# Delta rule on unnormalised queries and keys, with decay rows, grams, masks and weight units in another order

## The reference

```python
def l2_normalize(x):
    return x * lax.rsqrt(jnp.sum(x * x, axis=-1, keepdims=True) + EPS)

def gdn_direction(q, k, v, beta, g):
    gc = jnp.cumsum(to_chunks(g), axis=-1)
    decay = jnp.exp(jnp.where(incl, gc[..., :, None] - gc[..., None, :], -jnp.inf))
    kb = kc * bc[..., None]
    lower = jnp.where(strict, einsum("nbhid,nbhjd->nbhij", kb, kc) * decay, 0.0)
    rhs = jnp.concatenate([vc * bc[..., None], kb * jnp.exp(gc)[..., None]], axis=-1)
    sol = lax.linalg.triangular_solve(lower + eye, rhs, left_side=True, lower=True)
    ...
    # step over the chunks, with u, w = the two halves of sol
    v_new = ui - wi @ state
    out = (qi * exp(gi)) @ state + ((qi @ ki.T) * di) @ v_new
    state = state * exp(g_last) + (ki * exp(g_last - gi)).T @ v_new

q = l2_normalize(silu(conv(q))) * 128 ** -0.5;  k = l2_normalize(silu(conv(k)));  v = silu(conv(v))
o = o_f + o_b
o = o * lax.rsqrt(jnp.mean(o * o, axis=-1, keepdims=True) + EPS) * norm_g
```

## Time and profile before

| | |
|---|---|
| median of three runs | 1715.95 us |
| the profiled execution's own time | 1716.34 us |
| its span in the profile | 1714.5 us |
| PE busy | 1683.5 us (98%) |
| PE weight loads busy | 1386.5 us (81%) |
| DVE busy | 1160.8 us (68%) |
| ACT busy | 950.8 us (55%) |
| HBM read over the span | 289.05 MB |

### The profile page before, as it was taken

The page is one execution under the profiler, slowest core; times in us unless marked ns, Lnnn a source line. Parts: engine busy times, 40 slices in busy tenths (PEclk is TensorE's granted clock), DMA queues, the critical chain, the costliest instruction groups (busy, mean ns, idle before and its releaser), DMA issues.

```text
span 1714.5 us, 24757 instructions
## 1 busy us (share of the span) xinstructions
PE 1683.5 (98%) x10226; PEld 1386.5 (81%) x10226; DVE 1160.8 (68%) x1833; ACT 950.8 (55%) x1476; POOL 10.1 (1%) x22
## 2 busy tenths in 40 slices
PE   8999999999999999999999999999999999999998
PEld 6777888877778887888888888888888888878886
DVE  6976885679688667555686577655575556885554
ACT  7734644477155446444576767544564456974443
POOL 0000000000000000000000000000000000000000
PEclk9999999999999999999999999999999999999999
DMA  6322445542234555555544334655555555454553
GB/s 261 123 77 99 166 156 195 184 169 100 81 139 149 192 189 184 196 176 193 212 171 170 123 117 178 222 188 196 200 205 175 195 208 197 147 176 181 196 174 146
DMA packets 41872, 291.70 MB, mean 170 GB/s; under 512 B 4672, under 2 KB 4928, under 8 KB 7712
## 3 DMA queue, kind: packets, MB, share of 16 engines
q1 hardware_dynamic: 39312, 280.68, 45.6%
q0 software_dynamic: 2304, 8.91, 1.5%
q10 hardware_dynamic: 144, 0.52, 0.1%
HBM read 289.05 MB, written 1.05 MB: 169 GB/s over the span
## 4 chain that ended last, share of the span: by engine, by line
PE 81%; DVE 13%; ACT 3%; issue 2%; DMA 1%; SPq 0%; DVEq 0%; ACTq 0%
PE pg L477 24%; PE pg L479 24%; PE pg L478 24%; DVE wl L1985 3%; PE ps L846 2%; PE ps L665 2%; DMA raw<-weights 1%; ACT wh L1338 1%; PE ps L889 1%; PE ps L649 0%; PE ps L948 0%; PE ps L1233 0%; DVE hTl L2556 0%; PE ps L1188 0%; PE ps L1118 0%
## 5 line engine op out<-in xcount | busy, mean ns | idle before, releaser
L477 PE MATMUL pg<-wh,hTh 128*128 128x512 f32 x2092 | 833.2, 398 | 2.4 <-DVE hTl L2556 0.9
L479 PE MATMUL pg<-wh,hTl 128*128 128x512 f32 x2092 | 816.5, 390 | 0.0
L478 PE MATMUL pg<-wl,hTh 128*128 128x512 f32 x2092 | 815.4, 390 | 0.0
L1985 DVE TENSOR_TENSOR wl<-raw,wh 128x1024 fp32r<-128x1024 f32 x512 | 602.6, 1221 | 192.0 <-ACT wh L1338 188.7
L1338 ACT ACTIVATE wh<-raw 128x1024 fp32r<-128x1024 f32 x522 | 522.8, 1054 | 204.5 <-DMA raw<-weights 194.2
L477 PEld LDWEIGHTS pg<-wh,hTh 128*128 128x128 f32 x2092 | 393.2, 188 | 86.5 <-issue 8.3
L479 PEld LDWEIGHTS pg<-wh,hTl 128*128 128x128 f32 x2092 | 392.8, 188 | 84.0
L478 PEld LDWEIGHTS pg<-wl,hTh 128*128 128x128 f32 x2092 | 393.5, 188 | 75.1
L1444 ACT ACTIVATE arena<-pg,sm 128x256 f32<-128x256 f32 (+1 forms) x67 | 36.6, 546 | 239.9 <-PE pg L479 239.8
L2643 DVE SCALAR_TENSOR_TENSOR arena<-pg,sm,arena 128x256 f32<-128x256 f32 x88 | 38.5, 479 | 156.0 <-ACT arena L1445 156.0
L1404 ACT ACTIVATE hTh<-ps 128x512 fp32r<-128x512 f32 x60 | 33.6, 597 | 31.0 <-PE ps L665 31.0
(11 more groups left out here) (391 smaller groups left out, 1148.7 us busy)
## 6 DMA issues: line engine op xcount, KB each, us to landing
raw<-weights SPq DMA_DIRECT2D x265, 1024.0 KB, 4.8
arena<-wide POOLq DMA_DIRECT2D x9, 512.0 KB, 3.6
raw<-weights SPq DMA_DIRECT2D x2, 512.0 KB, 5.9
cst<-const_tables POOLq DMA_DIRECT2D x1, 1024.0 KB, 5.2
plainh<-dist_tables POOLq DMA_DIRECT2D x2, 512.0 KB, 5.7
arena<-gate_mix POOLq DMA_DIRECT2D x1, 1024.0 KB, 5.8
x<-x_in ACTq DMA_DIRECT2D x1, 512.0 KB, 4.0
x<-x_in SPq DMA_DIRECT2D x1, 512.0 KB, 9.2
```

Source lines behind the costliest of these rows:

```text
L477: pe.matmul(dst, lh, rh, start=first, stop=False)
L478: pe.matmul(dst, lh, rl, start=False, stop=False)
L479: return pe.matmul(dst, ll, rh, start=False, stop=last)
L1985: tt(wl[:, slot, h], raw[:, slot, h], wh[:, slot, h], ALU.subtract)\
```

## The change

- q and k are no longer normalised ahead of the products. `turn_back` leaves them in PSUM, the features of both are taken from the convolution's own output (which now lies where `qnT` and `knT` lie), so the second turn and its copies go; ACT copies the unnormalised k in rows. The norms of q and k are computed together (`norms`, 16 columns in place of 8 twice) and folded into small factors: beta times the key's norm into the values (in DVE's and ACT's hands), its product with the norm once more into BETAJ and NEGS, the query's norm into the last normalisation of o.
- The decay rows go to banks 0 and 1 ahead of the grams, and the grams to 2 and 3; the rows of cumulated sums and the turn of the small product move one chunk later or more.
- DVE's strict masks, a unit of weights and a split stand where the retention masks were. Retention's first mask terms are four ACT copies with a scale, among the inversion levels; DVE adds the second terms one by one (`both_ways`); the exponential moves behind the scan.
- The scaling of the inverse by beta goes. The outputs of the later visits go to a buffer of their own, added once at the end (`o_sum`). In the scan the splits are placed by hand.

The diff, cut to its core:

```diff
-        cvp = [V(8192), V(9216), V(10240)]
-        squares, qn = V(11264, 2048), V(13312)
+        cvp = [qnT, knT, V(10240)]
+        squares = V(12288, 2048)
...
 TensorE
                 def cumulated():
                     pe.wait_ge(sem["const_landed"], 16)
-                    c.wait("feat_read")
+                    c.wait("sq_ready")
                     c.wait("gate_g")
...
-                gemm(D, (512,), ("evac_act",), inside={(0, 2): first_turn, (0, 3): small_turned(16), (1, 3): first_back})
-                gemm(D, (512,), ("evac_act",), inside={(0, 1): second_turn, (1, 0): first_features, (1, 1): cumulated,
-                                                       (1, 3): back_and_rows})
-                prepare(2)
+                gemm(D, (512,), ("evac_act",), inside={(0, 2): first_turn, (1, 0): small_turned(16), (1, 3): first_back})
+                gemm(D, (512,), ("evac_act",), inside={(0, 1): second_turn, (1, 1): cumulated, (1, 3): second_back})
+                prepare(1)
+                cumulated_rows()
+                prepare(1)
                 c.wait("cum_t_read")
                 pe.wait_ge(sem["evac_act"], st.evacs["evac_act"])
                 turn(2)
-                prepare(3)
-                c.wait("qk_ready")
-                features(kn, 2)
-                prepare(3)
-                c.wait("feat_read")
+                prepare(6)
+                c.wait("sq_ready")
+                c.wait("kn_ready")
                 turn_back(2)
                 prepare(2)
                 c.wait("conv_read")
-                c.wait("back_read")
-                c.wait("v_read")
...
                 for j in range(8):
                     for r in range(2):
-                        last = pe.matmul(ps[half(r), 2 + j // 4, (j % 4) * P:(j % 4 + 1) * P],
+                        last = pe.matmul(ps[half(r), j // 4, (j % 4) * P:(j % 4 + 1) * P],
...
                 last.then_inc(sem["row_done"], 1)
+                c.wait("back_read")
+                c.wait("v_read")
...
                 c.wait("inv_scaled")
+                c.wait("vs_ready", 4)
...
 ScalarE
-                features(qnT, 0)
                 convolved(1)
                 square(1)
+                for m in range(M):
+                    last = act.activation(kn[:, 512 * m:512 * m + 512], ps[:, 2 + m, :], ACT.Copy)
+                last.then_inc(sem["kn_ready"], 1)
                 gemm(D, (512,), ("evac_act",), read(2))
...
-                features(knT, 2)
...
-                c.wait("mask_arg")
-                act.activation(MASKS, MASKS, ACT.Exp).then_inc(sem["mask_ready"], 1)
                 prepare(4)
                 act.activation(DELTA_Z, DELTA_Z, ACT.Silu).then_inc(sem["delta_z_ready"], 1)
+                c.wait("norms_ready")
                 for level in range(5):
                     prepare(1)
+                    if level < 4:
+                        t, d = ((0, 0), (1, 0), (2, 1), (3, 1))[level]
+                        m, r = scan_chunk(t, d)
+                        for h in range(NH):
+                            v, o = VS[half(r), t, h * P:(h + 1) * P], 8 * m + 4 * d + h
+                            last = act.activation(v, v, ACT.Copy, scale=BETA_NK[half(r), o:o + 1])
+                        last.then_inc(sem["vs_ready"], 1)
+                        if level == 0:
+                            act.wait_ge(sem["dist_landed"], 16 * (l + 1))
+                        act.activation(MASKS[:, 512 * level:512 * level + 512],
+                                       DIST.rearrange("p (s n) -> p s n", s=2)[:, 0, :], ACT.Copy,
+                                       scale=LAM[:, level:level + 1]).then_inc(sem["mask_first"], 1)
                     prepare(1)
...
-                c.wait("o_ready", 4)
+                c.wait("o_sum")
                 act.activation(Lm, o_acc, ACT.Square).then_inc(sem["sq_done"], 1)
+                c.wait("mask_arg")
+                act.activation(MASKS, MASKS, ACT.Exp).then_inc(sem["mask_ready"], 1)
...
 VectorE
+            def both_ways(h):
+                c.wait("mask_first")
+                RD = DIST.rearrange("p (s n) -> p s n", s=2)
+                mk = MASKS[:, 512 * h:512 * h + 512]
+                return stt(mk, RD[:, 1, :], LAM[:, 4 + h:5 + h], mk, ALU.mult, ALU.add)
...
+                def square_sums(t):
+                    c.wait("sq_ready")
+                    return dve.tensor_reduce((NQ, NK)[t], squares[:, 1024 * t:1024 * t + 1024]
+                                             .rearrange("p (k e) -> p k e", e=HD), AX.X, ALU.add)
+                def norms():
+                    c.step(square_sums(1))
+                    prepare(4)
+                    rstd_of(NORMS, 1.0)
+                    c.step(ts(NQ, NQ, HD ** -0.5, None, ALU.mult))
+                    tt(NQ2, NQ, NQ, ALU.mult)
+                    ...
+                    c.step(tt(by_direction(BETA_NK), by_direction(BETA), k_norms, ALU.mult))
+                    c.sig(tt(by_direction(BETA_NK2), by_direction(BETA_NK), k_norms, ALU.mult), "norms_ready")
+                    c.step(dve.tensor_copy(BETAJ..., BETA_NK2...))
-                normalized(0, qn)
...
-                normalized(1, kn)
+                square_sums(0)
                 gemm(D, (512,), ("evac_act",), ahead=2)
                 later_taps(2)
-                prepare(7)
+                norms()
                 c.wait("back_tr", 3)
                 for t, d in ((0, 1), (1, 1), (2, 0), (3, 0)):
-                    last = dve.tensor_copy(VS[half(r), t, :], ps[half(r), 2 + m, :])
+                    last = tt(heads(VS[half(r), t, :]), heads(ps[half(r), 2 + m, :]), over(BETA_NK[half(r), o:o + 4], P),
+                              ALU.mult)
                 last.then_inc(sem["v_read"], 1)
-                prepare(3)
...
+                c.wait("row_done")
+                tt(X3, ps[:, 0:2, :]..., over(GCJ, CHUNK), ALU.subtract).then_inc(sem["dist_ready"], 1)
                 for d, js in enumerate(both):
-                    tt(LM3[:, js, :], times(MASK["los" if d == 0 else "ups"], 8), over(BETAJ[:, js], CHUNK), ALU.mult)
-                c.wait("row_done")
-                tt(X3, ps[:, 2:4, :]..., over(GCJ, CHUNK), ALU.subtract).then_inc(sem["dist_ready"], 1)
-                retention_masks(l)
+                    last = tt(LM3[:, js, :], times(MASK["los" if d == 0 else "ups"], 8), over(BETAJ[:, js], CHUNK),
+                              ALU.mult)
+                c.step(last)
+                prepare(6)
                 c.wait("decay_ready")
                 c.step(tt(Lm, Lm, LMASK, ALU.mult))
...
                 c.sig(last, "low_ready")
-                prepare(4)
...
+                prepare(4)
...
+                    if s == 2:
+                        c.wait("cum_exp")
+                        ... six stt: NEGS = EGS * -1 * BETA_NK2, 64x4 each
                     if s < 32:
...
                         c.step(tt(XT3, XT3, xt_term, ALU.add))
+                        if i:
+                            c.step(both_ways(i - 1))
                         if s in (2, 8):
                             half_unit(1)
...
-                tt(TB3[:, 0:4, :], XT5[:, 0, 0], over(BETAJ[:, 0:4], CHUNK), ALU.mult)
-                ... three more such products
-                c.sig(last, "inv_scaled")
-                prepare(1)
-                prepare(1)
-                c.wait("cum_exp")
-                c.step(ts(NEGS, EGS, -1.0, None, ALU.mult))
+                c.sig(dve.tensor_copy(TB3[:, 4:8, :], ps[:, 1, 0:256]...), "inv_scaled")
+                visits = [v.rearrange("p (m e) -> p m e", m=M) for v in (o_acc, X_)]
                 for t in range(4):
...
-                    for _ in range(2 if t else 1):
-                        prepare(1)
                     if t:
-                        c.wait("ot_ready")
-                    if t >= 2:
-                        ... OT += O3 (two of 64x512)
+                        half_unit(0)
                     if t < 3:
                         ... the state, state_ready
-                        prepare(1)
+                    half_unit(1 if t else 0)
+                    if t:
+                        c.wait("ot_ready")
                     c.wait("sv_done")
                     ... outputs to visits[t // 2], o_ready
-                    prepare(1)
+                    if t == 0:
+                        half_unit(1)
+                        both_ways(3).then_inc(sem["mask_arg"], 1)
+                    prepare((5, 4, 4, 3)[t], 0)
...
             def delta_result():
+                c.sig(tt(o_acc, o_acc, X_, ALU.add), "o_sum")
                 pump(st.used + 3)
...
-                head_rstd(Lm, HD, STATS)
+                c.step(dve.tensor_reduce(STATS, Lm.rearrange("p (k e) -> p k e", e=HD), AX.X, ALU.add))
+                c.step(tt(STATS, STATS, NQ2, ALU.mult))
+                rstd_of(STATS, HD)
+                c.step(tt(STATS, STATS, NQ, ALU.mult))
```

(40 more changed lines are left out.)

68 lines of the change are left out of this document (22 added, 46 removed).

## The result

The changed kernel takes 1701.52 us (median of 5 runs, 1701.34 to 1702.61) against 1716.52 for the kernel before (5 runs on the same chip, 1715.75 to 1716.97): ratio 0.9913, 95% interval 0.9902 to 0.9924, 15.0 us less. The gain is 5.25 us larger than forecast (15.0 for 9.75); the 0.6 between 4.7 and 5.25 is the kernel before, 1716.52 here and 1715.95 in the forecast. The profiled execution took 1701.34 with a span of 1699.5.

The account below looks back on a forecast made before the run. TensorE's queue was taken to bound the kernel, so an edit is worth what it takes from its work or idle time. The terms sum to -9.75 us, giving a forecast of 1706.2 us, range 1702.0 to 1711.2.

Parts of the forecast that it names:

- part 7: Ahead of low_ready: mask operations leave DVE's way, so TensorE's wait at L855 goes, -2.8 us; inv_x comes earlier, -0.6.
- y: After the scan: o_sum and norm steps on DVE make y late, +0.35 us a layer, +0.7 in both.
- Parts 5 and 6: New TensorE waits: value turn on ScalarE's evacuation behind copies of k, +1.45 us; grams on DVE's scaled values, +2.2.
- Part 8: Inversion: both_ways at s=8 delays a DVE split and T3 of s=16, +0.4 us a layer, +0.8 in both.
- Part 9: Inversion's tail and scan: TensorE's waits at L897, L905 and L889 go, -0.9, -1.2 and -0.95 us.
- Part 2: small_turned one chunk later fills TensorE's wait for DVE's copy: -0.95 us in layer 0, nothing in layer 1.
- part 1: The 32 feature transposes of L740 go, with TensorE's idle time there: -4.8 us.
- Given back: Rival: the new waits eat the waits won behind them, only the transposes' gain is left, 1711.1 us; chance 0.13.
- Slower: Rival: weight splits run late in the scan and TensorE waits for them, 1719.8 us or above; chance 0.02.
- The clock: Rival: slow-clock stretch near the grams in both layers, 1707.8 us, chance 0.12; none, 1704.6; forecast keeps one.

Follow-up runs that it names:

- after_again: The changed kernel run once more, unchanged, for its profile: 1701.06 us.
- before_again: The kernel before run once more, unchanged, for its profile; no time of its own is given.
- f_v_act: Changed kernel with two of DVE's four scaled value copies given to ScalarE as plain copies, scaled later: 1698.05 us, ratio 0.9892.
- h_masks: Changed kernel with ScalarE's copies of k later, two value copies on ScalarE and both_ways(1) moved from s=8 to s=16: 1696.61 us, ratio 0.9883.
- b_small: Kernel before with only small_turned moved one chunk later: 1716.21 us, ratio 0.9999.
- u_small: Changed kernel with small_turned put back one chunk earlier, as in the kernel before: 1703.94 us.
- c_fill16: Changed kernel with 16 unread 8x8 filler products a layer ahead of the decay rows: 1704.41 us.

## Why the prediction was right and where it failed

**The step that failed** is the first: "the largest [wait], inside the block products, has no releaser ('issue') and isn't touched". It was touched, by the length of the stream. I took a wait without a releaser as a property of the work. It is 3.25 of the 5.25 us. With it the forecast would have been 1703.0. What the runs showed in its place: the gap is a late packet of instructions, and 16 products fewer a layer moved the place where PE needs it out of the dense products. Since I had no row on the fetch in the sum, the range had no case for it either; the lower end, 1702.0, was reached only by adding up other luck.

**What was mis-sized** makes up the other 2 us. The largest is part 7 with what belongs to it, 1.2 (next paragraph). y comes 0.25 late and not 0.7, the value turn costs 1.1 and not 1.45, the transposes gave 0.35 more with their starts. Against it stands 0.4 ahead of the first turn, which isn't the change's: `after_again` has that turn at 28.12 us and not at 28.63.

**Part 7 and the clock** were wrong in their terms, and the errors partly cancel. The forecast put L855's wait at 2.7 and counted 1.6 for the slow stretch at 76 us on both sides. `before_again`, without a stretch there, has L855 at 4.2, and PE's timeline is the same behind it (84.76 and 84.82). So in the kernel before the stretch cost nothing: PE ran 1.7 us slower and waited 1.5 less behind it. (The table puts these 1.5 to the clock.) Taking the wait away was worth 4.4 by the leads (2.2 a layer). A stretch in the changed kernel, now in layer 1 with no wait for `low_ready` behind it, costs 1.35 up to there. It gets 0.65 of that back at T3 of s=2: in the changed order PE waits some 0.5 there in every layer without such a stretch, and in none with one. That is the table's row of T3, no gain of the change. Together it is -3.7, where the forecast had -2.8; `inv_x` gave -0.85 and not -0.6.

**Parts 5 and 6** came as named, in place and size: 1.32 ahead of the grams with DVE's last value at 72.16, 0.54 ahead of the value turn in layer 1, though in layer 0 less (a wait of 0.21 for a weight split stands ahead of it now). The values' row of L2195 is 0.69 a piece, the plain copy's price that I had taken. `f_v_act` shows that part 6 was a real price and could be avoided. Part 8's slip is there with 0.32 and 0.31, and `h_masks` took it away. Part 9 was right within 0.15.

**Part 2 and part 1** were added up as if independent. On the kernel before they are not: `b_small` is worth 0.0 and not 0.95. The sum held because all parts went in at once, and DVE's first normalisation, which would have taken the gain back, went with them.

**The rivals.** "Given back" (1711.1) is out: the new waits took back 3.4 of what was won, and not all. "Slower" has nothing for it: PE waits for no split in the scan. "The clock": neither none nor two stretches but one, as in the forecast, though elsewhere. The Trainium skill's rule (TensorE: Matmul & The Clock Gate, section "What's actually happening"), that activity releases the clock from a throttled default, spoke for a stretch in both layers of the changed kernel. The runs agree in direction only: 7 in 10 layers with the wait, none in 8 of the same order without the wait and without thin fillers, but 3 in 4 with 16 thin fillers and at most 0.4 of wait, and the first layer of the changed kernel kept 2.4 GHz twice with its wait of 1.3.

## What to carry to other kernels

A wait with no releaser ("issue") inside dense short products is worth a look at the instruction queue. Count PE's records ahead of it: if gaps of several versions lie behind the same count, or a multiple of 256 apart, it is the fetch, and it moves or goes with any edit that changes the number of instructions ahead of it. An estimate should carry it as a case of its own (here 0 to 3.5 us). A wait that reads "issue" elsewhere can be an ordinary one (L759 on ScalarE's copy).

Before a slow-clock stretch or a wait is put in a sum, see whether the next wait absorbs it: price the two together, from a profile in which one of them is missing. And price small edits in their company: on a full in-order queue a part can be worth nothing alone (`b_small`) and its full size beside the part that clears the next wait (`u_small`).

## What was not expected of the hardware

Fillers of 8x8 that take PE under 1 us a layer cost up to 3.5 us in all through the fetch of instructions. PE stopped only where one packet of 256 instructions gives way to the next, and went on 2.2 to 2.5 us after that packet had started, in 20 gaps out of 20 (119.48 to 121.81, 446.41 to 448.90, 100.49 to 102.88, 421.41 to 423.87, ...).

Two profiles of the kernel before agree within 0.06 us at every piece of PE's timeline from 32 to 77 us, up to the slow stretch of the one, and again behind L855's wait. The slow stretches are nearly all that differs, and a kernel's medians hold them: in `c_fill16` the run with a mean clock of 0.996 took 1707.28, the one with 0.999 took 1703.33, while the four runs of `f_v_act`, all at 0.999, lie within 0.6 us. In a kernel this close to PE's bound, taking out an idle stretch ahead of thin products can give more than its own length (`f_v_act`: 3.5 us for waits of 2.6).
